# A hybrid decoder step: order of work in the mLSTM heads, and the queue of their state stores

## What is computed

```python
num = w_intra @ v + w_inter * (q @ C)
den = sum(w_intra) + w_inter * (q @ n)
h = num / max(abs(den), exp(-m_t))
C_new = decay * C + (k * w_state).T @ v
n_new = decay * n + sum(k * w_state)
```

## Time and profile before

| | us |
|---|---|
| median of 3 runs | 1140.9 |
| lowest and highest | 1136.46, 1145.33 |
| the profiled execution | 1138.19 |
| its span, first to last instruction | 1136.4 |
| TensorE busy in the span | 1076.2 (95%) |
| VectorE, ScalarE, GpSimd busy | 658.1, 545.2, 165.5 |

### The profile page before, as it was taken

How to read it: one execution, slowest core, us unless ns; L and a number is a source line. 1 busy time by engine, 2 the same in 40 slices (tenths; PEclk the granted TensorE clock), 3 DMA queues, 4 the chain that set the end, 5 groups by cost and what they waited for, 6 DMA issues and landing times.

```text
span 1136.4 us, 21540 instructions
## 1 busy us (share of the span) xinstructions
PE 1076.2 (95%) x8415; PEld 934.4 (82%) x8415; DVE 658.1 (58%) x954; ACT 545.2 (48%) x888; POOL 165.5 (15%) x212
## 2 busy tenths in 40 slices
PE   5999999789999999999999999999989999999995
PEld 5987878578999999998999855454638989999995
DVE  5567684623485553336996456868685386544333
ACT  5333655424456553425665344563643457553431
POOL 5224000000104220101401320200000104220100
PEclk9999999999999999999999999999999999999998
DMA  9799898998434444443742139898999434444431
GB/s 349 255 331 348 308 331 285 377 369 326 163 130 167 162 161 162 165 165 129 263 165 96 58 95 407 308 406 313 394 342 374 167 128 167 159 160 166 166 129 42
DMA packets 92585, 261.07 MB, mean 230 GB/s; under 512 B 8917, under 2 KB 9909, under 8 KB 92233
## 3 DMA queue, kind: packets, MB, share of 16 engines
q1 hardware_dynamic: 91642, 258.54, 62.5%
q0 software_dynamic: 432, 1.29, 0.4%
q10 hardware_dynamic: 432, 0.14, 0.0%
HBM read 218.21 MB, written 41.73 MB: 229 GB/s over the span
## 4 chain that ended last, share of the span: by engine, by line
PE 83%; DVE 10%; ACT 3%; issue 2%; DMA 1%; POOL 0%; SPq 0%; DVEq 0%; ACTq 0%; POOLq 0%
PE ps L2018 20%; PE ps L2020 20%; PE ps L2019 20%; PE ps L2130 2%; PE ps L2500 2%; PE ps L2211 2%; PE ps L2473 2%; PE ps L2375 2%; DVE cring L1733 2%; DVE w_lo L1208 1%; PE ps L2503 1%; PE ps L2419 1%; PE ps L2382 1%; DVE rstd L1238 1%; PE ps L2112 1%
## 5 line engine op out<-in xcount | busy, mean ns | idle before, releaser
L1208 DVE TENSOR_TENSOR w_lo<-w_raw,w_hi 128x1024 fp32r<-128x1024 f32 x232 | 286.3, 1240 | 217.3 <-ACT w_hi L702 216.0
L702 ACT ACTIVATE w_hi<-w_raw 128x1024 fp32r<-128x1024 f32 x232 | 242.2, 1054 | 209.2 <-PE ps L2020 174.6
L2018 PE MATMUL ps<-xin_hi,w_hi 128*128 128x288 f32 x1016 | 306.6, 302 | 15.9 <-DVE w_lo L1208 15.9
L2020 PE MATMUL ps<-xin_hi,w_lo 128*128 128x288 f32 x1016 | 303.6, 299 | 0.0
L2019 PE MATMUL ps<-xin_lo,w_hi 128*128 128x288 f32 x1016 | 303.2, 298 | 0.0
L2018 PEld LDWEIGHTS ps<-xin_hi,w_hi 128*128 128x128 f32 x1016 | 193.0, 190 | 28.2 <-DVE w_lo L1208 17.8
L2019 PEld LDWEIGHTS ps<-xin_lo,w_hi 128*128 128x128 f32 x1016 | 193.0, 190 | 0.6
L2020 PEld LDWEIGHTS ps<-xin_hi,w_lo 128*128 128x128 f32 x1016 | 192.4, 189 | 0.0
L2020 PE MATMUL ps<-hid_hi,w_lo 128*128 128x288 f32 x512 | 152.7, 298 | 0.0
L2019 PE MATMUL ps<-hid_lo,w_hi 128*128 128x288 f32 x512 | 151.4, 296 | 0.0
L2018 PE MATMUL ps<-hid_hi,w_hi 128*128 128x288 f32 x512 | 151.4, 296 | 0.0
(11 more groups left out here) (406 smaller groups left out, 1640.4 us busy)
## 6 DMA issues: line engine op xcount, KB each, us to landing
w_raw<-in_weights SPq DMA_DIRECT2D x232, 512.0 KB, 3.3
cring<-in_C SPq DMA_DIRECT2D x64, 512.0 KB, 6.4
out_Cs<-cring SPq DMA_DIRECT2D x64, 512.0 KB, 7.1
kv_a<-in_kv SPq DMA_DIRECT2D x52, 448.0 KB, 5.9
kv_b<-in_kv SPq DMA_DIRECT2D x52, 448.0 KB, 6.1
kv_w<-in_kv SPq DMA_DIRECT2D x24, 448.0 KB, 7.5
out_Cp<-cring SPq DMA_DIRECT2D x8, 512.0 KB, 6.4
out_v<-gaqkv SPq DMA_DIRECT2D x1, 1152.0 KB, 12.1
```

Source lines behind the costliest of these rows:

```text
L702: act.activation(w_hi[:, l % UM], w_raw[:, l % W_SLOTS], ACT.Copy).then_inc(hi_ready, 1)
L1208: dve.tensor_tensor(w_lo[:, l % W_SLOTS], w_raw[:, l % W_SLOTS], w_hi[:, l % UM], ALU.subtract).then_inc(lo_ready, 1)
L2018: pe.matmul(out, w_hi[:, j, ws], hi, start=start and kk == 0, stop=False)
L2020: last = pe.matmul(out, w_lo[:, l % W_SLOTS, ws], hi, start=False, stop=stop and kk == UK - 1)
```

## The change

- `ORDER` puts the prompt's halves behind batches 1 and 2. `outer` of them runs ahead of batches 2 and 3, `row_squares` and, for the next head, `head_rows` (now at batch 3) between the halves of those batches.
- For the next head, scores move from batch 7 to batch 5, ahead of the keys by token; `arguments` and exponentials to batch 4, `weights` and `queries` to batch 5. The sample values are made ahead of the values by token, and `USES` follows.
- `old_state(h, 1)` runs in batch 0 ahead of the numerators.
- VectorE's row gets places `between` the two new states of a batch and `behind` it: the skip lines and the keys' low part go between, the values' low part behind.
- Three products are cut by columns into groups of 32 partitions: the sample values' part, the group sum (its result `hs` is now 128 x 128), and the prompt's key sum in two rows, which makes one more store of `pack_n` at the end.
- Stores of the states are issued by GpSimd, 18 a head, each behind its own wait; row sums and the diagonals stand between them. SyncE keeps the loads.
- The samples' statistics, and in the last head the first two `w_lo`, move to other batches.

```diff
 ORDER = [(b, half) for b in range(NB) for half in range(2)]
-ORDER.insert(ORDER.index((2, 1)) + 1, (NB, 0))
-ORDER.insert(ORDER.index((3, 1)) + 1, (NB, 1))
+ORDER.insert(ORDER.index((1, 1)) + 1, (NB, 0))
+ORDER.insert(ORDER.index((2, 1)) + 1, (NB, 1))
...
-USES = ["q0", "q1", "q2", "q3", "k0", "k1", "k2", "k3", "kt0", "kt1", "ks", "vt0", "vt1", "vs",
-        "bc0", "bc1", "sc", "n", "mean"]
+QK = ["q0", "q1", "q2", "q3", "k0", "k1", "k2", "k3"]
+KEYS_V = ["kt0", "kt1", "ks", "vs", "vt0", "vt1"]
+USES = [(h, name) for h in range(NH) for name in
+        [*([] if h else QK + KEYS_V), "bc0", "bc1", *([] if not h else QK), "sc", *([] if not h else KEYS_V), "n", "mean"]]
...
-            def c_store(i):
...
-                sp.wait_ge(*made(i))
...
-                sp.dma_start(dst[:, HD2 * half:HD2 * half + HD2], cring[s]).then_inc(c_out[s], 16)
...
                 if i == (NH - 1) * ITEMS:
-                    sp.wait_ge(stage_full, use(NH - 2, "vs") + 1)
+                    sp.wait_ge(stage_full, use(NH - 2, "vt1") + 1)
...
-                c_store(i)
...
             def values_by_token(h):
+                src = staged(h, "vs")
+                act.activation(vtk_s, src[0:NS], ACT.Copy)
+                act.activation(vst[:, h % 2], src[0:3 * NS], ACT.Copy).then_inc(vst_hi_ready, 1)
                 for tt in range(2):
                     src = staged(h, f"vt{tt}")
                     act.activation(vtk[:, tt], src, ACT.Copy)
                     act.activation(vw[:, tt], src, ACT.Copy, scale=tokg[:, tt, NH + h:NH + h + 1]
                                    ).then_inc(stage_read_a, 1)
-                src = staged(h, "vs")
-                act.activation(vtk_s, src[0:NS], ACT.Copy)
-                act.activation(vst[:, h % 2], src[0:3 * NS], ACT.Copy).then_inc(vst_hi_ready, 1)
...
-                if b in (2, 3):
+                if b in (1, 2):
                     if h + 1 == NH:
-                        act_hi(b - 2, 0, STEP0[OUT_C])
-                    prompt_state(h, b - 2)
+                        act_hi(b - 1, 0, STEP0[OUT_C])
+                    prompt_state(h, b - 1)
+                if b == 3 and h + 1 < NH:
+                    head_rows(h + 1)
                 if b == 4 and h + 1 < NH:
                     qk(h + 1)
+                    exps(h + 1)
...
+                if b == 7:
                     if h == 2:
                         sample_high(0)
-                if b == (6 if h + 1 < NH else 4):
-                    act.wait_ge(y1_full, h + 1)
-                    act.activation(y1_hi[:, ET * h:ET * h + ET, 0:SEQ], hT, ACT.Copy).then_inc(y1_hi_ready, 1)
-                if b == 7:
                     act.wait_ge(hs_psum, h + 1)
                     act.activation(hs4, ps[:, 2, :], ACT.Copy).then_inc(hs_copied, 1)
                     if h + 1 < NH:
-                        head_rows(h + 1)
+                        own_values(h + 1, 0)
 
                     act.wait_ge(hs_sum, h + 1)
-                    act.activation(hs[:, h], ps[0:NS, 3, :], ACT.Copy).then_inc(hs_taken, 1)
+                    act.activation(hs[:, h % 2], ps[:, 3, 0:P], ACT.Copy).then_inc(hs_taken, 1)
                     act.wait_ge(hs_taken, h + 1)
-                    act.activation(hs_junk, hs[:, h], ACT.Square, accum_out=stok[:, 1, h:h + 1]).then_inc(hs_sq, 1)
-                    if h + 1 < NH:
-                        exps(h + 1)
+                    act.activation(hs_junk, hs[:, h % 2], ACT.Square, accum_out=stok_a[:, 1, h:h + 1]).then_inc(hs_sq, 1)
...
-                dve.tensor_copy(nrows[N_P:N_P + 1, h], pn[N_P:N_P + 1]).then_inc(stage_read_v, 1)
+                for r in range(2):
+                    row = slice(N_P + NS * r, N_P + NS * r + 1)
+                    es = slice(DH // 2 * r, DH // 2 * r + DH // 2)
+                    last = dve.tensor_copy(nrows[row, h, es], pn[row, es])
+                last.then_inc(stage_read_v, 1)
...
+                if b == 3:
+                    order.wait()
+                    dve.wait_ge(z_ready, h + 1)
+                    dve.tensor_tensor(hT, hT, z[:, ET * h:ET * h + ET, 0:SEQ], ALU.mult).then_inc(y1_full, 1)
+                if b in (4, 5) and h + 1 == NH:
+                    dve_lo(b - 4, 0, STEP0[OUT_C])
+                if b == 4 and h + 1 < NH:
+                    arguments(h + 1)
+                if b == 6 and h == 2:
+                    sample_rows(0)
+                if b == 5 and h + 1 < NH:
+                    weights(h + 1)
+                    queries(h + 1)
+                if b == 7 and h == 2:
+                    sample_low(0)
+                if b == 6:
...
+                    dve.wait_ge(y1_hi_ready, h + 1)
+                    dve.tensor_tensor(y1_lo[:, ET * h:ET * h + ET, 0:SEQ], hT, y1_hi[:, ET * h:ET * h + ET, 0:SEQ],
+                                      ALU.subtract).then_inc(y1_ready, 1)
+            def between(h, b):
+
                 if b == 3:
                     order.wait()
                     for e in range(ET):
...
+                if b == 6 and h + 1 < NH:
                     keys_low(h + 1)
+
+            def behind(h, b):
+
                 if b == 6 and h + 1 < NH:
                     values_low(h + 1)
...
-                if b == 7:
-                    if h + 1 < NH:
-                        queries(h + 1)
-                        arguments(h + 1)
-                        weights(h + 1)
...
-                    for half in range(2):
-                        new_state(h, b, half)
+                    new_state(h, b, 0)
+                    between(h, b)
+                    new_state(h, b, 1)
                     chunk(h, b)
+                    behind(h, b)
...
+            def c_store(i):
+
+                h, r = divmod(i, ITEMS)
+                b, half = ORDER[r]
+                s = i % C_SLOTS
+                pool.wait_ge(*made(i))
+                dst = O["Cs"][b, h] if b < NB else O["Cp"][h]
+                dst = dst.rearrange("(t p) e -> p t e", p=P)
+                pool.dma_start(dst[:, HD2 * half:HD2 * half + HD2], cring[s]).then_inc(c_out[s], 16)
...
-                if h + 1 < NH:
-                    if h >= 1:
-                        pool.wait_ge(stage_full, use(h - 1, "vs") + 1)
-                    head_diagonals(h + 1)
-                row_sums(h)
+                for r in range(ITEMS):
+                    c_store(ITEMS * h + r)
+                    if r == 1:
+                        row_sums(h)
+                    if 2 <= r < 5 and h + 1 < NH:
+                        if h >= 1:
+                            pool.wait_ge(stage_full, use(h - 1, "vt1") + 1)
+                        diagonals_of(h + 1, r - 2)
...
             def values_by_token(h):
+                samples_thrice(h, "vs", 2, lambda m: xms[:, m])
                 for tt in range(2):
                     by_token(h, f"vt{tt}", 2, lambda m: xm[:, m, PAD + P * tt:PAD + P * tt + P])
-                samples_thrice(h, "vs", 2, lambda m: xms[:, m])
...
-                    last = pe.matmul(out[N_P:N_P + 1], tokg[:, tt, NH + h:NH + h + 1], ktok[:, tt],
-                                     start=False, stop=tt == 1, skip_group_check=True)
+                    for r in range(2):
+                        row = slice(N_P + NS * r, N_P + NS * r + 1)
+                        es = slice(DH // 2 * r, DH // 2 * r + DH // 2)
+                        last = pe.matmul(out[row, es], tokg[:, tt, NH + h:NH + h + 1], ktok[:, tt, es],
+                                         start=False, stop=tt == 1, skip_group_check=True)
...
-                pe.matmul(ps[0:NS, 3, :], four_eyes, hs4, start=True, stop=True).then_inc(hs_sum, 1)
+                for e in range(ET):
+                    last = pe.matmul(ps[NS * e:NS * e + NS, 3, 0:P], four_eyes, hs4[:, P * e:P * e + P],
+                                     start=True, stop=True, skip_group_check=True)
+                last.then_inc(hs_sum, 1)
...
-                    pe.matmul(ps[0:NS, 2, :], ew[0:NS, 3 * P:3 * P + NS], vtk_s, start=False, stop=False,
-                              skip_group_check=True)
+                    for e in range(ET):
+                        pe.matmul(ps[NS * e:NS * e + NS, 2, P * e:P * e + P], ew[0:NS, 3 * P:3 * P + NS],
+                                  vtk_s[:, P * e:P * e + P], start=False, stop=False, skip_group_check=True)
+                    old_state(h, 1)
                     numerators(h)
...
                     if b == 4:
                         qk(h + 1)
                     if b == 5:
+                        scores(h + 1)
                         keys_by_token(h + 1)
                     if b == 6:
                         values_by_token(h + 1)
                     if b == 7:
-                        head_rows(h + 1)
                         sum_groups(h)
-                        scores(h + 1)
...
-                    last = old_state(h, b)
+                    if b != 1:
+                        last = old_state(h, b)
                     if b == NB - 1:
```

(27 more changed lines are left out.)

65 lines of the change are left out of this document (26 added, 39 removed).

## The result

The changed kernel takes 1144.5 us (median of 20 runs, 1140.2 to 1151.3) where the kernel before takes 1139.2 (1135.0 to 1145.3) on the same chips: the ratio is 1.0046, with a 95% interval of 1.0031 to 1.006. It is slower by some 5 us, where a gain of 4.7 us, to 1133.5, was named. The stated range of 1120 to 1146 holds the measured time, but the change went the other way. The profiled execution of after took 1143.4 us, with a span of 1141.3.

A forecast was written before the change was run, and what follows sets the result against it. The prediction took TensorE's own work plus small waits to bound three of four heads, and VectorE the last. Savings of 3.9 us there and 0.8 in the last head, with stores at 0, gave 1138.2 - 4.7 = 1133.5 us; range 1120 to 1146.

The forecast's parts named there:

- What bounds the kernel: Three of four heads bound by TensorE's own work plus small waits, 50.7 us each; VectorE sets the last head's pace.
- The work that goes: Cutting sample values, group sum and prompt's key sum on TensorE saves 0.7, 0.74 and 0.86, together 2.3 us a head.
- The waits: TensorE's old waits, 2.8 us a head, go; two new waits for VectorE cost 3.8 us a head.
- the 0.9 of batch 4: TensorE waits 0.9 us in batch 4, as VectorE's skip lines stand between batch 3's two new states.
- the 2.9 of batch 6: TensorE waits 2.9 us at the second token tile for VectorE's low part of the values; bounds 0 to 3.7.
- 49.4 was forecast: Period from one head's first denominator matmul to the next's: 49.4 us.
- what they were to be balanced by: In the third head, the moved sample work spares TensorE about the price of the sample rows.
- rival 3: TensorE at half clock for 5 us behind each 2.9 us gap: 7.5 us more, 1141 us; chance 0.10.
- stores on GpSimd's queue: 0: GpSimd has room for 18 stores a head, and loads a few us later cost nothing: 0 us.
- rival 2: Transfers in two queues become the bound, from 351 GB/s and less; at 301 GB/s, 1154 us; chance 0.16.
- -3.9 for three heads: Saving of 1.3 us a head in three heads: 5.1 saved by work and waits against 3.8 of new waits.
- -0.8 in the last head: Last head gains 0.8 us from a shorter start, partly given back by VectorE's own work; bounds 0 and 3.

The follow-up runs named there:

- e6: The changed kernel with 11 unread 128-column products put on TensorE where it waits in batch 6 of heads 0 and 1; 1143.0 us, ratio 1.0012.
- e1: The changed kernel with VectorE's low part of the values ahead of the sample rows and y1_lo in batch 6; 1139.1 us, ratio 0.9998.
- e5: The kernel before with only the three cut products, orders otherwise untouched and stores on SyncE's queue; 1141.9 us, ratio 1.0018.
- e3: The changed kernel with the stores of the new states back on SyncE's queue; 1142.9 us, ratio 1.0028.
- e4: The kernel before with its stores of the new states moved to GpSimd's queue, diagonals and row sums spread between them; 1142.6 us, ratio 1.0034.
- e2: The changed kernel with the values in the old order on TensorE and ScalarE, token tiles first and samples last; 1136.5 us, ratio 0.9972.
- e8: e2 with the stores on SyncE's queue; 1130.1 us, ratio 0.9901.
- e9: e8 with VectorE's keys' low part ahead of batch 6's first new state and the skip lines behind batch 3's second; 1125.2 us, ratio 0.9879.

## Why the prediction was wrong

**What bounds the kernel.** Right for heads 0 to 2: TensorE's own row and its waits for VectorE. No wait for a load stands there in after.

**The work that goes.** Forecast 0.7 + 0.74 + 0.86 = 2.3 us a head; by the starts of the rows in after and before about 0.6 + 0.7 + 0.85 = 2.15. The mode changes cost nothing that the rows show. The drain of which the Trainium skill, "TensorEngine Tiling (Array Packing)", Key Properties, speaks isn't seen here as time: behind the cut sample values, 0.42 us from 718.66, the next row begins at 719.01.

**The waits.** Forecast 2.8 us a head gone and 3.8 new. In the second head of after 3.5 us of waits are left (0.20 + 0.60 + 0.68 + 2.00) where before has 3.1. By the forecast it would be 4.1: the 0.9 of batch 4 came as 0.60, the 2.9 of batch 6 as 0.68 + 2.00. Work and waits alone would make the period 50.7 - 2.15 + 0.4 = 48.95. From that to 51.12 it is 2.2 us: 1.6 of half clock and 0.5 for the sample values and the two token tiles, which take 3.3 us where before has 2.85 now that waits stand between them; the rest is small. Without the half clock it would be 49.5, where 49.4 was forecast, so the step on the waits holds. In the third head the sample rows lengthen the gap to 2.8 us, and what they were to be balanced by falls short.

**The step that failed first** is the one that took the granted clock as full behind the gap, rival 3, with a chance of 0.10. It came in every head. In the second it is 0.77 us more for the old state and 0.82 for the outer products, 1.6 us; in the third it is 0.92 for the second token tile and 0.52 for the old state. The period became 51.1 us and not 52, as the half clock held for less than the 5 us I had named. The argument against it was too thin: gaps of 1.06 and 0.64 us that left the clock full said nothing about one of 2.0. e6 shows the mechanism, and e1 that it goes with the gap. Gaps of up to 1.25 us in the middle of dense work left the clock full (e5, with the prompt's product behind it in 3.70 us); no run was made to find the limit.

**The second** is the term "stores on GpSimd's queue: 0". The slack of a single load was read rightly and was not the question. What mattered was how many bytes the engines move in a head, and the price stood in the last head, where I had expected a gain of 0.8 us: 3.1 us of waits for loads in after. By the medians the queue cost 1.7 us in after (e3, with overlapping intervals), 3.3 in before (e4) and 6.4 in e2 (e8); only the last is far outside the noise. It is rival 2's mechanism at a rate of 373 GB/s and not 301. That rate clears rival 2's threshold of 351, and so the first three heads run free, but it leaves a debt. An issue took 0.73 us by its rows, not 0.57; no run shows what that alone is worth.

**The sum.** From -3.9 for three heads it became 0.42 + 0.42 + 1.21 = +2.05 against before, from -0.8 in the last head +2.05, and the projection behind it, begun at half clock, took 0.9 us longer (4.24 for its first step, before 3.37). Head 0 began 0.4 us sooner. That makes 4.6 of the 4.9 us between the two spans; the other 0.3 lie further behind. That the time is inside the stated range is luck and no merit of the sum, as the range's upper part was put in for rival 2, by which the transfers bound every head.

**What the change could have brought.** Its order and its cuts are worth 1% together (e8), once the values keep their old order and the stores their old queue; with two more lines of VectorE moved it is 1.2% (e9).

## What to carry to other kernels

Where an in-order engine waits in the middle of dense work, price a gap of 2 us at more than its length: work behind it may run at half clock, so ask first whether the gap can be filled or split. Where work is taken out of the busiest engine, check what that engine waits for next, since the same cuts were worth about 0.5% here in one order and nothing in the other. And read a queue's slack as bytes a head against the rate with both kinds of transfer running, up to the last consumer, not as the margin of one load.

## What the runs showed of the hardware

- Eleven matmuls without a reader, put into the gap, made the two heads that had them 1.3 us shorter each, since they kept TensorE's clock at 2.4 GHz.
- Half clock can begin behind the gap with a delay: behind 2.00 us of idling the first eight matmuls took 1.16 us as at full clock, and the old state after them 1.83 where it takes 1.06.
- The clock can fall without a long gap: in e5 TensorE idled 0.17 us ahead of the scores, and they ran at 1.2 GHz. In before's second head the same row, behind a group sum of 1.05 us, ran at 2.4. And equal rows can differ: behind 0.3 us of idling the third head's group sum and scores took 1.04 and 2.89 us in before, 1.83 and 3.74 in e4.
- The 16 DMA engines moved 399 GB/s at a share of 1.05 with loads and stores in one queue, and 372 at 1.01 with the stores in GpSimd's. In short stretches two queues reached 410 as well (784 to 804 us of e2: 411), so the difference is not one of the peak.
